# Two layers' expert entry: the last projection quarter in two pieces, and the picked rows formed in transposed order

## The chip, the cores and the metric

One Trainium2 chip, one of its cores. The metric is the device time of one launch in microseconds (us). The kernel before takes 2126.44 us (median of 3 runs, 2125.73 to 2127.97).

## The reference, cut to what matters

The program is two stacks of layers in one launch, all in fp32. The change touches only the second stack (256 latent tokens and 256 context tokens of width 1024, two layers), and in each of its layers only the passage from the mixer to the mixture of experts:

```python
# per layer: y_lat is the mixer's output (MLA in layer 0, short convolution in layer 1)
x = x + g1 * y_lat                                   # y_lat = heads @ w_o   (256 x 1024 @ 1024 x 1024)
f = rmsnorm(x) * g * (1 + sc2) + sh2
g_prob   = softmax(f @ w_group)                      # 4 groups
g_sel    = argmax(g_prob + b_group)
e_logits = (f @ w_expert)[g_sel]                     # 8 experts in the chosen group
e_prob   = softmax(e_logits); top-2 of e_prob + b_expert
# each token goes to 2 of 32 experts, whose weights are 3 x (1024 x 512) each:
y_e = (silu(f @ w_gate[e]) * (f @ w_up[e])) @ w_down[e]
x = x + g2 * sum over the two experts of weight * y_e
# after the second layer: rmsnorm(x) * final_g is the output (256 x 1024)
```

In both layers only the latent rows (256 tokens, so 512 assignments) go through the experts here, and all 32 experts' weights are read, 6 MB each.

## The kernel before, in words

**Entry** (`entry` in each engine's program, once per layer). The product with `w_o` is made in four quarters (token tile c of 128 rows, half h of 512 columns), each 8 matmuls deep, in order (0,0), (0,1), (1,0), (1,1), in banks 0 to 3. VectorE multiplies each quarter by the gate row and adds it to the residual (L2379, L2380). TensorE transposes the new rows of a quarter (`rows_T`, through `tr`, L870), ScalarE squares them for the norm (L1659) and copies the transposed rows to `hT` (L1836). The router's logits (`logits(c)`, 8 matmuls of 36 columns) need all of a tile's columns. In the last quarter (1,1) TensorE does, between its 4th and 5th k, the transpositions of (1,0) and the logits of tile 0 (`beside`). After the last quarter come its transpositions and the logits of tile 1. VectorE then has the two sums of squares added, the root, a diagonal `zdiag` for the normed rows of tile 1 (L2393), and from the logits (L2414, L2415) runs the routing, a chain of some 50 small instructions, up to the one-hot matrices of the first round (L2497, L2504).

**Experts** (`experts`). The 512 assignments are put in 48 blocks of 32 slots, each block of one expert; a round takes 3 blocks, so there are 16 rounds per layer. Turn b of TensorE is: gate product and up product (8 k each; of every k three matmuls of 32 stationary columns run side by side on the array, L1277 and L1279), forming of the next round's rows (`rows_of(b + 1)`, L1250: the one-hot matrix, 96 columns, is stationary and 512 columns of the normed tokens `fN` move; 2 halves x 2 token tiles, 4 matmuls, 8 records), transposition of the hidden rows (L1308), down product (4 k x 2 halves), and between its 2nd and 3rd k the transposition of the next round's rows (`rows_T(b + 1)`, L1261, 8 transpositions). The formed rows are copied from PSUM to `xe` in halves, one by ScalarE (L1791) and one by VectorE (L2492). The weights come straight from memory, where partition p holds rows 8p to 8p+7 of gate and up (4p to 4p+3 of down). So the stationary operand of chunk k has to hold the columns k, k+8, k+16, ... of the formed rows, and `rows_T` takes every eighth column of `xe` (`"t (p k) -> t k p"`) as the operand that is loaded: its words lie 32 bytes apart. The hidden rows (L1308) are read every fourth, 16 bytes apart. One product of the first stack also loads its weights with a stride: the compression takes `u[:, 0:31, j]`, words 64 bytes apart (the 128*31 loads of L856), while the 128*30 loads read `hid`, neighbouring words. No instruction of the kernel before moves an operand with a stride between its words.

**Weights of the experts.** Three experts lie in SBUF (`experts3`). SP issues 1 MB halves in a fixed order and waits before each for the quarter of the product that frees its place (`again`, L781). ScalarE and VectorE copy the weights of the second and third block of a round to a side buffer, a quarter at a time (L1780, L2538). The first round of a layer: rows formed, copied and transposed as a whole, then both copied to `xeT` (L1761), then the turn.

## Time and profile before

| | before |
|---|---|
| median of 3 runs | 2126.44 us |
| the profiled execution's own time | 2125.36 us |
| its span | 2123.5 us, 29332 instructions, mean granted clock 0.978 |
| PE busy | 1984.4 us (93%) |
| DVE busy | 992.9 us (47%) |
| ACT busy | 682.4 us (32%) |
| DMA moved | 619.89 MB, 292 GB/s on average |
| chain that ended last | PE 68%, DMA 24%, DVE 3%, ACT 2% |

Busy time is the union of an engine's instructions. The chain is followed back from the last instruction, at each step to what released it. The two layers of the second stack take the stretch from about 968 us to the end: entry and routing of layer 0 at 968 to 1002, its 16 rounds to 1478, the convolution and entry of layer 1 to 1632, its rounds to 2109.

### The profile page before, as it was taken

Reading aid. Unit: us, or ns where it says so; the run is one execution under the profiler, and the core shown is the slowest. Engines: PE = TensorE matmul, PEld = TensorE weight load, DVE = VectorE, ACT = ScalarE, POOL = GpSimd, SP = SyncE. Lnnn points to the kernel's source line nnn. Section 1 sums busy time; section 2 is a strip of 40 time slices with the busy share of each in tenths; the row PEclk is TensorE's granted clock in tenths of the full one; section 3 lists DMA queues with packets and bytes.
Section 4 is the critical chain, followed back from the end, with each engine's and each line's share of the span. In section 5 each row is a group of like instructions: output and inputs, shape, how many; then the busy total and the mean of one; then the engine's idle time right before and its main releaser. Section 6 shows DMA issues by size and latency. Waiting matters only on the chain.

```text
span 2123.5 us, 29332 instructions
## 1 busy us (share of the span) xinstructions
PE 1984.4 (93%) x9625; PEld 1080.3 (51%) x9626; DVE 992.9 (47%) x2203; ACT 682.4 (32%) x1092; POOL 45.0 (2%) x80
## 2 busy tenths in 40 slices
PE   8999999999999999999999888889998999888887
PEld 4536777646577775554433333334774333333333
DVE  2566886303398543444444333335224444333335
ACT  1451000103400003142555444444103554444444
POOL 2000000000000000000000000001000000000000
PEclk9999999998999999999999999999999999999999
DMA  9507995433289443305899999999555999999996
GB/s 306 210 7 290 362 346 220 159 119 140 106 343 366 149 165 136 122 37 201 351 414 422 419 416 422 423 423 367 218 198 210 400 419 423 422 423 422 422 422 256
DMA packets 78655, 619.89 MB, mean 292 GB/s; under 512 B 9664, under 2 KB 10000, under 8 KB 15712
## 3 DMA queue, kind: packets, MB, share of 16 engines
q1 hardware_dynamic: 67968, 540.51, 63.4%
q0 software_dynamic: 6944, 66.35, 8.2%
q10 hardware_dynamic: 3648, 11.89, 1.4%
q8 instruction: 44, 0.72, 0.1%
q14 instruction: 51, 0.42, 0.1%
HBM read 605.08 MB, written 13.63 MB: 291 GB/s over the span
## 4 chain that ended last, share of the span: by engine, by line
PE 68%; DMA 24%; DVE 3%; ACT 2%; issue 1%; DVEq 0%; SPq 0%; ACTq 0%; POOL 0%; POOLq 0%
PE ps L856 26%; DMA big<-in_w_up 21%; PE ps L1277 14%; PE ps L1103 14%; PE ps L1115 7%; PE ps L870 2%; PE ps L1250 2%; PE ps L1279 2%; DMA big<-in_w_gate 1%; DMA big<-in_w_down 1%; ACT big L1780 1%; PE ps L1261 1%; DMA big<-in_first_final_g 0%; DMA big<-in_dense 0%; PE ps L1125 0%
## 5 line engine op out<-in xcount | busy, mean ns | idle before, releaser
L1277 PE MATMUL ps<-big,hT 128*32 128x512 f32 x3072 | 698.2, 608 | 81.8 <-ACT big L1780 66.8
L1279 PE MATMUL ps<-big,hT 128*32 x1536 | 697.0, 608 | 0.0
L1780 ACT COPY big<-big 128x1024 f32 x384 | 395.6, 1046 | 494.2 <-PE ps L1279 269.6
L2538 DVE TENSOR_SCALAR big<-big 128x1024 f32 x384 | 262.1, 692 | 437.4 <-PE ps L1279 301.7
L1277 PEld LDWEIGHTS ps<-big,hT 128*32 128x32 f32 x3072 | 189.0, 111 | 459.9 <-issue 254.3
L1103 PE MATMUL ps<-hT,big 128*128 128x256 f32 x1408 | 311.2, 379 | 0.0
L856 PE MATMUL ps<-big,hT 128*128 128x512 f32 (+4 forms) x784 | 302.1, 537 | 3.4 <-ACT hT L1719 2.1
L1103 PEld LDWEIGHTS ps<-hT,big 128*128 128x128 f32 x1408 | 266.7, 190 | 49.4 <-issue 15.2
L856 PEld LDWEIGHTS ps<-big,hT 128*128 128x128 f32 x784 | 139.2, 192 | 131.7 <-issue 123.4
L1279 PEld LDWEIGHTS ps<-big,hT 128*32 128x32 f32 x1536 | 158.3, 111 | 3.7
L1115 PE MATMUL ps<-big 128*128 128x512 f32 x352 | 159.3, 595 | 0.7 <-DVE big L2302 0.7
L856 PE MATMUL ps<-big 128*128 128x512 f32 (+15 forms) x636 | 141.0, 451 | 13.8 <-issue 5.3
L2312 DVE SCALAR_TENSOR_TENSOR big<-big,s_ccol 128x512 f32<-128x512 f32 x196 | 147.4, 752 | 7.0
L1744 ACT ACTIVATE big<-big 128x256 f32<-128x256 f32 x44 | 18.3, 417 | 367.3 <-DVE big L2294 367.3
L1250 PE MATMUL ps<-big,hT 128*96 128x512 f32 x256 | 118.1, 604 | 1.2 <-DVE hT L2504 1.2
L856 PE MATMUL ps<-hT,big 128*128 128x256 f32 (+1 forms) x480 | 113.2, 397 | 1.9 <-ACT hT L2021 1.9
L856 PEld LDWEIGHTS ps<-big 128*128 128x128 f32 (+8 forms) x636 | 69.7, 176 | 79.8 <-issue 64.3
L856 PEld LDWEIGHTS ps<-hT,big 128*128 128x128 f32 x480 | 92.3, 193 | 23.7 <-issue 11.9
L1115 PEld LDWEIGHTS ps<-big 128*128 128x128 f32 x352 | 66.1, 190 | 73.5 <-issue 69.0
L2276 DVE TENSOR_TENSOR big<-ps,big 128x512 f32<-128x512 f32 x44 | 30.4, 690 | 115.4 <-PE ps L1103 114.6
L1250 PEld LDWEIGHTS ps<-big,hT 128*96 128x96 f32 x256 | 39.3, 163 | 78.0 <-issue 76.7
L2572 DVE TENSOR_TENSOR hT<-hT,ps 96x512 f32<-96x512 f32 x32 | 21.9, 683 | 88.6 <-PE ps L1279 88.6
(331 smaller groups left out, 1258.9 us busy)
## 6 DMA issues: line engine op xcount, KB each, us to landing
big<-in_w_gate SPq DMA_DIRECT2D x128, 1024.0 KB, 23.7
big<-in_w_up SPq DMA_DIRECT2D x128, 1024.0 KB, 23.2
big<-in_w_down SPq DMA_DIRECT2D x128, 1024.0 KB, 21.7
big<-in_dense SPq DMA_DIRECT2D x52, 1536.0 KB, 8.7
big<-in_dense POOLq DMA_DIRECT2D x28, 2048.0 KB, 9.9
big<-in_dense SPq DMA_DIRECT2D x20, 2048.0 KB, 7.9
y_rows<-c_res ACTq DMA_DIRECT2D x30, 384.0 KB, 7.0
big<-in_dense SPq DMA_DIRECT2D x7, 1024.0 KB, 31.7
```

What stands on the lines that cost most here:

```text
L856: ins = nc.tensor.matmul(out, lhsT, rhs, start=start, stop=stop)
L870: ins = nc.tensor.transpose(out, rows, const["ident"][0:k, 0:k])
L1103: ins = nc.tensor.matmul(ps[:, t % 2, f * S:(f + 1) * S], w[:, k, f * P:(f + 1) * P], hT[:, k, S:2 * S], start=k == 0, stop=k == KT - 1)
L1115: ins = nc.tensor.matmul(ps[:, 4 + 2 * c + h, :], gT[:, t % 2, c * P:(c + 1) * P], w[:, h * BW:(h + 1) * BW], start=t == 0, stop=t == FT - 1)
L1250: ins = nc.tensor.matmul(ps[0:ROWS, h, :], onehot[:, t, :], fN[:, t, h * BW:(h + 1) * BW], start=t == 0, stop=t == T - 1)
L1277: nc.tensor.matmul(ps[g * SLOTS:(g + 1) * SLOTS, bank, :], xT[:, k, g * SLOTS:(g + 1) * SLOTS], side[:, g - 1, quarter % 2, at:at + BW], s ...
L1279: return nc.tensor.matmul(ps[0:SLOTS, bank, :], xT[:, k, 0:SLOTS], experts3[:, bass.ds(here, 1), kind * CH + row:kind * CH + row + BW] .re ...
L1780: nc.scalar.copy(side[:, 1, quarter % 2, :], experts3[:, bass.ds(there, 1), lo:lo + QW] .rearrange("p a n -> p (a n)")).then_inc(s["side2_ ...
L2276: tt(U[:, par, :, 2:S + 2], ps[:, par, :].rearrange("p (a b) -> p a b", a=2), token_scale, mult)\
L2312: ins = stt(acc, mod_w[j % 2][:, k, :], ccols[:, k, col:col + 1], acc, mult, add)
L2538: ts(side[:, 0, quarter % 2, :], experts3[:, bass.ds(there, 1), lo:lo + QW].rearrange("p a n -> p (a n)"), 1.0, None, mult).then_inc(s["si ...
L2572: tt(hm[0:ROWS, :], sgm[0:ROWS, :], ps[0:ROWS, 3, :], mult).then_inc(s["hidden_done"].sem, 1)
```

## The change

The last quarter of the projection becomes two pieces of 256 columns, so that `PIECES` has five entries (tile, first column, width). TensorE makes piece 3, then the transpositions of piece 2 and the logits of tile 0 (both of its pieces), then piece 4 with the transpositions of piece 3 between its 6th and 7th k, then the logits of pieces 2 and 3, the transpositions of piece 4 and its logits. ScalarE squares and copies by pieces, VectorE adds the sums of squares of pieces 2 and 3 early and that of piece 4 in one instruction. `zdiag` moves behind the first two instructions of the routing.

In every round of the experts the rows are formed in transposed order: the 512 columns of `fN` that move are now four runs of 128 words, each run with a stride of 8 words (32 bytes), and `xe` is filled so that `rows_T` loads 128 neighbouring words for each transposition. `rows_T` waits for the two copied halves one after the other. In the first round of a layer ScalarE copies its half of the formed rows before its first copy of weights, VectorE its half after one copy of weights instead of two, and the turn begins when the first half of the transposed rows is there; the second half is awaited before k = 4.

```diff
...
 
+        PIECES = [(0, 0, BW), (0, BW, BW), (1, 0, BW), (1, BW, BW // 2), (1, BW + BW // 2, BW // 2)]
+        PIECE_BANKS = (0, 1, 2, 3, 2)
...
-                def product(c, h, between=None):
+                def product(i, between=None, at=4):
+                    c, lo, n = PIECES[i]
                     for k in range(KT):
-                        if between is not None and k == 4:
+                        if between is not None and k == at:
                             between()
-                        mm(ps[:, 2 * c + h, :], lhs(k, c), w[h][:, k, :], k == 0, k == KT - 1,
+                        mm(ps[:, PIECE_BANKS[i], 0:n], lhs(k, c), w[lo // BW][:, k, lo % BW:lo % BW + n], k == 0, k == KT - 1,
                            s["banks_ready"].sem if k == KT - 1 else None)
 
-                def rows_T(c, h):
-                    pe.wait_ge(s["dve_evac"].sem, s["dve_evac"].at(2 * c + h + 1))
-                    for k in range(4):
-                        tr(ps[:, 4 + 2 * c + h, k * P:(k + 1) * P], lat(c)[:, (4 * h + k) * P:(4 * h + k + 1) * P],
-                           e["turn_ready"].sem if k == 3 else None)
-
-                def logits(c):
-                    for k in range(KT):
-                        if k % 4 == 0:
-                            pe.wait_ge(e["turned_a"].sem, e["turned_a"].at(2 * c + k // 4 + 1))
+                def rows_T(i):
+                    c, lo, n = PIECES[i]
+                    pe.wait_ge(s["dve_evac"].sem, s["dve_evac"].at(i + 1))
+                    for k in range(n // P):
+                        tr(ps[:, PIECE_TURNS[i], k * P:(k + 1) * P], lat(c)[:, lo + k * P:lo + (k + 1) * P],
+                           e["turn_ready"].sem if k == n // P - 1 else None)
+
+                def logits(i):
+                    c, lo, n = PIECES[i]
+                    pe.wait_ge(e["turned_a"].sem, e["turned_a"].at(i + 1))
+                    for k in range(lo // P, (lo + n) // P):
                         mm(ps[:, c, 0:G + E], hT[:, k, S + c * P:S + (c + 1) * P], wrG[:, k, :], k == 0, k == KT - 1,
                            r["route_pe"].sem if k == KT - 1 else None)
 
                 def beside():
-                    rows_T(1, 0)
+                    rows_T(2)
                     logits(0)
-
-                product(0, 0)
+                    logits(1)
+
+                product(0)
                 pe.wait_ge(r["route_dve"].sem, r["route_dve"].at(1))
                 mm(ps[:, 3, 0:G + E], const["ones"][:], swS, True, True, r["route_pe"].sem)
-                product(0, 1)
-                rows_T(0, 0)
-                product(1, 0)
+                product(1)
+                rows_T(0)
+                product(2)
                 used()
-                rows_T(0, 1)
+                rows_T(1)
                 pe.wait_ge(r["route_dve"].sem, r["route_dve"].at(2))
-                product(1, 1, beside)
+                product(3)
+                beside()
+                product(4, lambda: rows_T(3), 6)
                 used()
-                rows_T(1, 1)
-                logits(1)
+                logits(2)
+                logits(3)
+                rows_T(4)
+                logits(4)
...
@@ -1247,17 +1260,17 @@
                         pe.wait_ge(s["xT_done"].sem, s["xT_done"].at(b * 2))
                     for h in range(2):
                         for t in range(T):
-                            ins = nc.tensor.matmul(ps[0:ROWS, h, :], onehot[:, t, :], fN[:, t, h * BW:(h + 1) * BW],
+                            ins = nc.tensor.matmul(ps[0:ROWS, h, :].rearrange("t (k p) -> t k p", k=4), onehot[:, t, :],
+                                                   fN[:, t, :].rearrange("t (p k) -> t k p", k=KT)[:, 4 * h:4 * h + 4, :],
                                                    start=t == 0, stop=t == T - 1)
                         ins.then_inc(s["rows_ready"].sem, 1)
 
                 def rows_T(b):
 
-                    pe.wait_ge(s["rows_copied_a"].sem, s["rows_copied_a"].at(b + 1))
-                    pe.wait_ge(s["rows_copied_v"].sem, s["rows_copied_v"].at(b + 1))
-                    for h in range(2):
+                    for h, copied in enumerate((s["rows_copied_a"], s["rows_copied_v"])):
+                        pe.wait_ge(copied.sem, copied.at(b + 1))
                         for k in range(4):
-                            rows = xe[0:ROWS, :].rearrange("t (p k) -> t k p", k=KT)[:, 4 * h + k, :]
+                            rows = xe[0:ROWS, (4 * h + k) * P:(4 * h + k + 1) * P]
                             ins = nc.tensor.transpose(ps[:, h, k * ROWS:(k + 1) * ROWS], rows,
                                                       const["ident"][0:ROWS, 0:ROWS])
                         ins.then_inc(s["xT_ready"].sem, 1)
@@ -1287,12 +1300,14 @@
                 def turn(b, first=False, more=True):
 
                     here = pe.value_load(tab_i[0:1, 0, bass.ds(b * WIDE, 1)], min_val=0, max_val=BPE - 1)
-                    pe.wait_ge(s["xT_done"].sem, s["xT_done"].at(b * 2 + 2))
+                    pe.wait_ge(s["xT_done"].sem, s["xT_done"].at(b * 2 + (1 if first else 2)))
                     if not first:
                         pe.wait_ge(s["hidden_done"].sem, s["hidden_done"].at(b))
                     for kind in range(2):
                         for quarter in range(4):
                             both_copied(b, 4 * kind + quarter)
+                            if first and kind == 0 and quarter == 2:
+                                pe.wait_ge(s["xT_done"].sem, s["xT_done"].at(2))
                             for k in range(2 * quarter, 2 * quarter + 2):
...
@@ -1755,8 +1770,8 @@
                 s = st[name]
                 done = s["quarter_done"]
 
-                def rows_T(b):
-                    for h in range(2):
+                def rows_T(b, halves=range(2)):
+                    for h in halves:
                         act.wait_ge(s["xT_ready"].sem, s["xT_ready"].at(b * 2 + (h + 1)))
                         nc.scalar.copy(xeT[:, 4 * h:4 * h + 4, :], ps[:, h, 0:4 * ROWS].rearrange("p (a b) -> p a b", a=4))\
...
                 there = third(0)
+                row_half(0)
                 copy(0, there, 0)
-                row_half(0)
+                rows_T(0, (0,))
                 copy(0, there, 1)
-                rows_T(0)
+                rows_T(0, (1,))
                 for b in range(ROUNDS):
...
-                            .then_inc(e["turned_a"].sem, 1)
+                for i, (c, lo, n) in enumerate(PIECES):
+                    act.wait_ge(s["dve_evac"].sem, s["dve_evac"].at(i + 1))
+                    nc.scalar.activation(sq_rest[:, min(i, 3), lo % BW:lo % BW + n], lat(c)[:, lo:lo + n], ACT.Square,
+                                         accum_out=ssq_pieces[:, i:i + 1]).then_inc(e["squares_done"].sem, 1)
+                    if i == 1:
+                        root_of(0)
+                    act.wait_ge(e["turn_ready"].sem, e["turn_ready"].at(i + 1))
+                    nc.scalar.copy(hT[:, lo // P:(lo + n) // P, S + c * P:S + (c + 1) * P],
+                                   ps[:, PIECE_TURNS[i], 0:n].rearrange("p (a b) -> p a b", b=P))\
+                        .then_inc(e["turned_a"].sem, 1)
                 root_of(1)
...
-                for c in range(TC):
-                    for h in range(2):
-                        i = 2 * c + h
...
+                def sum_of(i):
+                    v.wait_ge(e["squares_done"].sem, e["squares_done"].at(i + 2))
+                    link(v, tt(sums[:, 0:1], ssq_pieces[:, i:i + 1], ssq_pieces[:, i + 1:i + 2], add))
+                    link(v, ts(var[:, 0:1], sums[:, 0:1], 1.0 / D, EPS, mult, add))
+
+                for i, (c, lo, n) in enumerate(PIECES):
...
+                    v.wait_ge(s["banks_ready"].sem, s["banks_ready"].at(i + 1))
+                    link(v, tt(prodO[:, i % 2, 0:n], ps[:, PIECE_BANKS[i], 0:n], gate_row[layer][:, cols], mult))
+                    tt(out, out, prodO[:, i % 2, 0:n], add).then_inc(s["dve_evac"].sem, 1)
+                    if i == 2:
+                        link(v, stt(fN[:, 0, :], lat(0), rstd_x[:, 0:1], rowG, mult, mult))
...
-                ts(zdiag, const["ident"][:], rstd_x[:, 1:2], None, mult).then_inc(e["zdiag_done"].sem, 1)
+                        v.wait_ge(s["dve_evac"].sem, s["dve_evac"].at(i + 1))
+                        link(v, tt(fN[:, 1, cols], out, rowG[:, cols], mult))
+                    if i == 1:
+                        sum_of(0)
+                        root_of(e, 0, rstd_x[:, 0:1])
+                    if i == 3:
+                        sum_of(2)
+                nc.vector.memset(lg[:, 0:TC, G:], NEG)
+                v.wait_ge(e["squares_done"].sem, e["squares_done"].end)
+                link(v, stt(var[:, 0:1], ssq_pieces[:, 4:5], 1.0 / D, var[:, 0:1], mult, add))
+                root_of(e, 1, rstd_x[:, 1:2])
...
                 L(red(top, lg, ALU.max))
                 tt(ae, lg, wide(top, EPG), sub).then_inc(step, 1)
+                e = st["ent" + tag]
+                ts(zdiag, const["ident"][:], rstd_x[:, 1:2], None, mult).then_inc(e["zdiag_done"].sem, 1)
                 v.wait_ge(s["route_act"].sem, s["route_act"].end)
...
                         copy(b, there, loads, j, first)
-                        if j == 1 and first:
+                        if j == 0 and first:
                             row_half(s, 0)
```

## Rows read from the trace of the kernel before

**Rows 1.** Chain of waits, its longest pieces: start us, us, what

```profile
...
1025.21 3.60 PE ps L1250 x8
...
1051.67 3.60 PE ps L1250 x8
...
1440.77 3.60 PE ps L1250 x8
...
1453.42 17.30 DMA big<-in_w_down
...
1654.02 3.60 PE ps L1250 x8
...
2071.46 3.60 PE ps L1250 x8
...
```

**Rows 2.** Windows of layer 0: us, busy of each engine, PE clock, DMA share, GB/s

```profile
core 0: us, PE busy (x) PEld busy (x) DVE busy (x) ACT busy (x) POOL busy (x), PEclk, DMA share, GB/s
1010.00:1013.00 3.00, 3.00 (x18) 1.74 (x15) 0.68 (x1) 0.65 (x1) 0.00 (x0) 0.66 0.00 0
1020.00:1130.00 110.00, 108.36 (x683) 41.69 (x680) 48.27 (x85) 59.02 (x67) 0.00 (x0) 1.00 1.01 413
1330.00:1440.00 110.00, 96.18 (x588) 42.01 (x588) 42.51 (x75) 49.84 (x56) 0.00 (x0) 0.97 1.01 423
```

**Rows 3.** Groups of all instructions by shape: busy us, mean ns of one, idle before

```profile
...
L1250 PE MATMUL ps<-big,hT 128*96 128x512 f32 x256 | 118.1, 604 | 1.2 <-DVE hT L2504 1.2
...
L2921 DVE TENSOR_TENSOR big<-big,ps 128x256 f32<-128x256 f32 x8 | 3.4, 422 | 69.1 <-PE ps L856 69.1
...
```

**Rows 4.** Groups of weight loads by shape

```profile
...
L1261 PEld LDWEIGHTS ps<-c_ident,c_res 96*128 96x128 f32 x256 | 31.0, 204 | 28.7 <-issue 26.8 <-ACT c_res L1791 1.9
...
L870 PEld LDWEIGHTS ps<-c_ident,c_res 128*128 128x128 f32 x48 | 5.5, 140 | 2.1 <-issue 2.1
...
L856 PEld LDWEIGHTS ps<-big 128*31 128x31 f32 x64 | 2.4, 138 | 1.2 <-issue 0.4
...
L856 PEld LDWEIGHTS ps<-big 128*30 128x30 f32 x4 | 0.2, 107 | 0.8 <-issue 0.8
...
```

**Rows 5.** Timeline of a later round, the transpositions' weight loads

```profile
...
1033.22 0.97 PEld L1261 LDWEIGHTS ps<-c_ident,c_res 96*128 96x128 f32 x8 [0.84 <-issue]
...
```

**Rows 6.** Timeline of layer 1's entry: start us, us, instruction, idle before

```profile
...
1611.31 3.68 PE L856 MATMUL ps<-big 128*128 128x512 f32 x8
...
1615.10 0.69 DVE L2379 TENSOR_TENSOR big<-ps,big 128x512 f32<-128x512 f32 x1 [4.93 <-PE ps L856]
...
1616.55 0.63 ACT L1659 ACTIVATE big<-x_res 128x512 f32<-128x512 f32 x1 [6.16 <-DVE x_res L2380]
...
1617.06 1.92 PE L856 MATMUL ps<-big,hT 128*128 128x36 f32 x16
...
1618.70 0.29 DVE L2393 TENSOR_SCALAR big<-c_ident,rstd_x 128x128 f32<-128x128 f32 x1
...
1619.19 0.21 DVE L2414 SCALAR_TENSOR_TENSOR big<-ps,rstd_x,big 128x4 f32<-128x4 f32 x1
...
```

**Rows 7.** Timeline of layer 0's entry, the last logits

```profile
...
987.27 2.75 PE L856 MATMUL ps<-big,hT 128*128 128x36 f32 x16
...
990.06 0.22 DVE L2414 SCALAR_TENSOR_TENSOR big<-ps,rstd_x,big 128x4 f32<-128x4 f32 x1 [0.57 <-PE ps L856]
...
```

**Rows 8.** Timeline of layer 0's first round

```profile
...
1001.83 3.67 PE L1250 MATMUL ps<-big,hT 128*96 128x512 f32 x8 [1.16 <-DVE hT L2504]
...
1005.43 0.57 ACT L1791 COPY c_res<-ps 96x512 f32<-96x512 f32 x1
...
1005.74 0.68 DVE L2492 COPY c_res<-ps 96x512 f32<-96x512 f32 x1
...
1006.57 1.10 PE L1261 MATMUL ps<-c_ident,c_res 96*128 96x96 f32 x8 [1.07 <-DVE c_res L2492]
...
1008.46 0.94 PE L1277 MATMUL ps<-big,hT 128*32 128x512 f32 x2 [0.78 <-ACT hT L1761]
...
```

**Rows 9.** Timeline of layer 1's first round

```profile
...
1637.28 1.10 PE L1261 MATMUL ps<-c_ident,c_res 96*128 96x96 f32 x8 [0.87 <-DVE c_res L2492]
...
1638.96 0.62 PE L1277 MATMUL ps<-big,hT 128*32 128x512 f32 x2 [0.58 <-ACT hT L1761]
...
```

45 lines of the change are left out of this document (13 added, 32 removed).

## The prediction

> **What bounds the kernel now.** I read the chain of waits first. Through the experts of both layers it runs over TensorE's rounds at first and over the landing of weights later: rounds begin every 26.46 us at the start (1025.21 to 1051.67), while over 14 rounds the mean is (1440.77 - 1025.21) / 14 = 29.68 us in layer 0 and (2071.46 - 1654.02) / 14 = 29.82 us in layer 1 [rows 1]. The windows tell why. From 1020 to 1130 TensorE is busy 108.4 of 110 us, from 1330 to 1440 only 96.2 of 110, with the DMA engines fully busy at 423 GB/s [rows 2]. So transfers bound most rounds, and TensorE has 3.3 us to spare in a mean round and none in the first four or five. Two places are not covered by transfers. Between a layer's entry and its first round the DMA has nothing to do: 0 GB/s from 1010 to 1013, because the three places for experts are full until the first round frees one [rows 2]. What comes earlier there shifts the whole stream of transfers. The other is the last round: in layer 0 the chain still waits for w_down until 1453.42 + 17.30 = 1470.7, in layer 1 it is on TensorE from 2071.46 on [rows 1].
>
> The working is against the profiled execution, 2125.36 us (span 2123.5 and 1.9 around it), which stands 1.1 us under the median of 2126.44; differences carry over to the median unchanged.
>
> **Entry, both layers.** TensorE's order before the last piece is the same work: piece 3 and the first half of the old quarter both take 8 x 512 columns' time, since 16 records of 256 columns stand for 8 of 512, and the transpositions and 16 logit records between are the same. After the last product (ends 1611.31 + 3.68 = 1614.99) the old path is two VectorE instructions of 0.69 (1615.10 on), the squares (0.63, from 1616.55), the sums, the root, `zdiag` (0.29) and the logits' reading, of which the second tile's begins at 1619.19: 4.2 us [rows 6]. The new path: 256 columns take VectorE 0.42 instead of 0.69 [rows 3], twice, -0.54; the squares of 256 instead of 512 columns, -0.21 at the same proportion (an estimate); one small sum less, -0.19 (estimate, the spacing of such instructions); `zdiag` now runs where VectorE waits for ScalarE's exponential, about -0.2. Sum -1.1. The logits don't stand in the way: of the 16 records of 1617.06 (1.92 us) [rows 6] only the last 4 are left after the last copy, about 0.5 us, and they end near 1617.8, before the root. In layer 0 the old path also waited 0.57 for those logits, 2.75 us long at a lower clock [rows 7]; I take -1.5 there. Bounds: from 0 (the root alone sets the time and nothing shrinks) to -2.0. The second chunk of the projection's weights is also given back earlier, which only brings forward transfers whose data is not awaited.
>
> **First round, both layers.** Old, layer 0: rows formed 1001.83 to 1005.50, VectorE's copy to 1006.42, 8 transpositions from 1006.57, ScalarE's two copies, products from 1008.46 [rows 8]. New with rows formed at the old pace: VectorE's copy starts 0.1 earlier, at 1005.6, its transpositions run at 1006.4 to 1006.8 and TensorE goes straight on, since the first half is copied by then: products from 1006.9, -1.55. Layer 1: VectorE's copy already begins as the rows end; the transpositions of the second half end near 1637.7 and products start then instead of at 1638.96 [rows 9], -1.2. ScalarE's copy of weights moves behind its row copy by 0.57 [rows 8]; it is wanted at the first product, which leaves it 0.8 us. If that cover were gone it would cost at most those 0.57.
>
> **Rows formed by strided reading, 32 rounds.** Here the trace has no row of its own: no operand moves with a stride. The nearest rows are weight loads. A transposition's load of 128 neighbouring words takes 140 ns, of 128 words 32 bytes apart 204 [rows 4]: 0.50 ns more a word. For a product, which goes in fp32 at 2 cycles of the clock a word, 30 neighbouring words take 107 ns and 31 words 64 bytes apart 138 [rows 4]: about 0.97 ns more a word, twice the other. That is what a reader that fetches every word twice, and pays each time, would show. The moving side of the same product also takes 2 cycles a word: 8 records of 512 in 3.67 us [rows 3, 8], 0.43 us from one to the next. Paid twice a word it costs 512 x 0.97 = 0.50 us a record, 4.0 us for the 8 of a round. From throughput: 8 strided loads in 0.97 us, the last of them 0.20 long, are 0.110 us apart [rows 5], 0.86 ns a word; twice that is 0.88 us a record against 0.43, 3.6 us a round. Paid once, 0.25 a record, 2.0 a round. If the reader is fast enough for a word every two cycles, nothing. I take 3.5, near the product's own loads, and keep 0 and 4.0 for the range. The saving on the other side, 8 contiguous loads instead of strided ones, is at most 8 x 0.064 = 0.5 us a round and more likely 0.1, since the loads run beside the transpositions.
>
> The Trainium skill, "Advanced Engine Details and Errata", SBUF Cachelines, says that an access on another 16-byte line each time pays a penalty, and that two hits on a line are enough to absorb the latency. The rows on loads agree with the first half. By the second half, a record that fetches each word twice in a row would pay nothing; the 31-word load, if it fetches twice in a row, speaks against that. What it would make of the time is the first rival below.
>
> **What 3.5 us a round costs.** In the first round of each layer all of it is on the path. The start of the products then stands at -1.5 - 1.55 + 3.5 = +0.45 in layer 0 and -1.1 - 1.2 + 3.5 = +1.2 in layer 1. A TensorE-bound round becomes 26.3 + 3.5 - 0.1 = 29.7 to 29.9 us, against the means of 29.68 and 29.82: the slack of later rounds is gone, though little of the time is lost directly, 14 x 0.1 = 1.5 in layer 0, 0 in layer 1. With both at one pace each hiccup of either costs. In the TensorE-bound stretch transfers ran at 413 GB/s and not 423 [rows 2], 2.4% lost; if that held for some 340 us more of each layer, it were 8 us a layer. I take 2.5 a layer, 5 in all (bounds 0 and 16). In the last round the forming of round 15's rows at 2071.46 is on the path in layer 1: +3.5; in layer 0 it eats first what the wait for w_down leaves, +1.8 of 3.5. Sum: 0.45 + 1.2 + 1.5 + 5 + 1.8 + 3.5 = +13.5, so 2138.9 for the profiled execution and **2140** for the median. Its own range is 2130 (no coupling, and a price of 2.8) to 2153.
>
> **Rivals.**
> *The stride is free.* The words arrive in time for a 2-cycle pace. For it: three products run side by side on the array, so SBUF gives far more words than one stream asks; loads may have a shallower reader. Against it: the 31-word load. Then each layer's start shift is the whole effect, because the transfers follow it: -1.5 - 1.55 - 1.1 - 1.2 = -5.35, and the rounds' small saving is hidden under transfers: 2126.4 - 5.3 = 2121, range 2118 to 2123.5. This is the side of faster; it decides below a price of about 1 us a round.
> *Paid once a word.* 2.0 a round: first rounds -1.05 and -0.3; rounds of 28.2 stay under the transfers' 29.7; last rounds +2.0 and +0.5. Sum +1.2, 2127.5, range 2124 to 2130.
> *The halves don't do what they say.* If the second half's copy or ScalarE's later weight copy holds the first products, 1.0 us of each first round's gain is lost: +2 on any case; it changes no sign of the first and is in the ranges.
> *Coupling is hard.* With both servers at one pace and transfers issued strictly in order, 8 us a layer instead of 2.5: 2150, the top of the forecast's own range.
>
> **Chances.** The forecast (stride paid twice, with hard coupling in it) 0.56, free 0.31, once 0.13. What a measurement can tell from no change is 0.2%, 4.3 us: faster is under 2122.2, slower over 2130.7. The forecast is slower in 92 of 100 of its cases; free is faster in 87; once is mostly within. Slower 0.56 x 0.92 + 0.13 x 0.25 = 0.55, faster 0.31 x 0.87 + 0.02 = 0.29, same 0.16. For 8 in 10 the range takes in most of the free case: 2119 to 2151; the forecast's own is 2130 to 2153.
>
> **What would show it.** The records that form the rows: 0.43 us apart (free), 0.68 (once), 0.88 (twice), 8 of them 3.7, 5.5 or 7.2 us. The transpositions' loads at about 140 ns. The first products of a layer after its last rows record: 1.4 us instead of 3.0. From the end of the last product to the second tile's logits: 3.1 us instead of 4.2. TensorE-bound rounds of 29.8 instead of 26.4 and transfers over 1020 to 1130 below 413 GB/s. The prediction is wrong if the records keep their 592 ns, or if rounds lengthen and the layers' lengths don't: then transfers covered more than I count.

## The result, and the profile after

The changed kernel takes **2156.41 us** (median of 4 runs, 2151.95 to 2160.33) against 2126.96 for the kernel before, run beside it (2125.73 to 2127.97): slower by 29.5 us, a ratio of 1.0147 (95% interval 1.0125 to 1.0168). The forecast was slower, by 13.5 us, in a range from 2119 to 2151: the direction was right and the size was not. The profiled execution took 2160.33 us (span 2158.5), 4 us above its median.

First the price of the strided reading. These are the groups of all instructions by shape in the changed kernel (busy us, mean ns of one, idle before), which answer to [rows 3, 4]:

```profile
L1263 PE MATMUL ps<-big,hT 128*96 128x512 f32 x256 | 241.9, 1102 | 2.3 <-DVE hT L2527 2.3
...
L1274 PEld LDWEIGHTS ps<-c_ident,c_res 96*128 96x128 f32 x256 | 22.6, 141 | 29.4 <-issue 28.1 <-DVE c_res L2515 1.3
```

A record that forms rows takes 1102 ns instead of 604, and the loads of the transpositions 141 instead of 204. Then the chain of waits, the pieces that answer to [rows 1]:

```profile
1032.30 7.49 PE ps L1263 x8
...
1212.42 7.49 PE ps L1263 x8
1242.38 7.49 PE ps L1263 x8
...
1461.93 7.49 PE ps L1263 x8
...
1680.80 7.49 PE ps L1263 x8
...
2102.68 7.49 PE ps L1263 x8
```

The 8 records of a round take 7.49 us where they took 3.60, and a TensorE-bound round is 1242.38 - 1212.42 = 29.96 us long instead of 26.34. Fourteen rounds last 1461.93 - 1032.30 = 429.6 us in layer 0 (before 415.6) and 2102.68 - 1680.80 = 421.9 in layer 1 (before 417.4). Where in a layer the time goes is seen in windows cut where the rows of rounds 1, 8 and 15 are formed. The columns are the window's length, the busy time of each engine, PE's clock, the DMA share and GB/s. First the kernel before, the first two windows in layer 0, the last two in layer 1:

```profile
1025.10:1221.80 196.70, 186.32 (x1149) 73.18 (x1148) 83.30 (x147) 99.11 (x112) 0.00 (x0) 0.98 1.01 416
1221.80:1440.70 218.90, 192.62 (x1150) 84.07 (x1149) 83.38 (x147) 98.29 (x112) 0.00 (x0) 0.97 1.01 421
1654.00:1850.30 196.30, 186.05 (x1150) 74.95 (x1149) 83.18 (x147) 98.90 (x112) 0.00 (x0) 0.99 1.01 418
1850.30:2071.40 221.10, 192.73 (x1150) 84.47 (x1149) 83.29 (x147) 98.15 (x112) 0.00 (x0) 0.97 1.01 422
```

Then the same rounds of the changed kernel:

```profile
1032.20:1242.30 210.10, 208.54 (x1149) 70.06 (x1148) 83.28 (x147) 100.15 (x112) 0.00 (x0) 1.00 0.96 390
1242.30:1461.90 219.60, 211.96 (x1152) 74.92 (x1149) 83.56 (x147) 99.44 (x112) 0.00 (x0) 0.99 1.01 417
1680.70:1890.50 209.80, 208.23 (x1149) 68.14 (x1148) 83.28 (x147) 100.13 (x112) 0.00 (x0) 1.00 0.99 404
1890.50:2102.60 212.10, 209.06 (x1151) 70.26 (x1148) 83.35 (x147) 99.84 (x112) 0.00 (x0) 1.00 1.01 422
```

The loss stands in the first seven rounds of the stretch, 13.4 us in layer 0 and 13.5 in layer 1. There TensorE is now busy for 99% of the time, and the transfers drop from 416 to 390 GB/s and from 418 to 404. The work moved is the same in layer 0 (416 x 196.7 and 390 x 210.1 are both 82 MB). The later seven rounds take 0.7 us more in layer 0; in layer 1 they take 9.0 less, at 422 GB/s both times. There the transfers had run ahead: 404 x 209.8 is 84.8 MB against 418 x 196.3 = 82.1 before, and 2.7 MB are 6.4 us at 422 GB/s. Layer 1's chain of waits stays on TensorE up to 2040, so most of its later rounds are bound by TensorE too, at 29.96 us each. What sets the layers apart is mostly one round, layer 0's from 1212.4; this is it, and the same round of layer 1:

```profile
1212.40:1242.40 30.00, 29.79 (x167) 9.75 (x166) 11.90 (x21) 14.30 (x16) 0.00 (x0) 1.00 0.83 328
1860.70:1890.60 29.90, 29.69 (x165) 9.62 (x165) 11.89 (x21) 14.30 (x16) 0.00 (x0) 1.00 1.01 422
```

In layer 0's, the queue that issues the weights waits 18.7 us at one stretch for a place in SBUF that TensorE's products free; in layer 1's it is 8.9 us at most.

The rest of the profiled difference: 3.5 us lie ahead of layer 0's entry, where no instruction differs. I put them down to this execution: the traces of experiments 2, 3 and 4, with the same instructions up to there, stand 2.0 us later, 3.8 later and 0.6 earlier than the kernel before. From the first rows to the second rows of a layer it is +3.5 (26.85 against 23.31) and +5.0 (26.73 against 21.70); behind the last rows of layer 1 +3.8. The entry gained nothing in layer 0 and 1.7 us in layer 1. But the 1.7 us are not the shorter path of the pieces. Counted from the entry's first transposition, layer 1's products that count the experts' rows start at 26.83 us, before at 26.88; the gain lies behind them, 5.69 us to the first rows instead of 7.38, where the kernel before ran at half clock (1.2 of 2.4 GHz). First that stretch before, then in the changed kernel; the eighth number is the granted clock:

```profile
1626.80:1631.50 4.70, 4.68 (x8) 2.09 (x8) 3.32 (x20) 0.59 (x1) 0.00 (x0) 0.50 1.01 427
1649.90:1653.90 4.00, 2.94 (x16) 1.50 (x16) 3.40 (x20) 1.17 (x2) 0.00 (x0) 1.00 1.01 428
```

This stretch takes 6.4 to 7.4 us in layer 1 in the traces with the old entry (the kernel before and experiments 1, 5, 6, 7, 9 and 10) and 5.7 to 5.9 in those with the new one (the changed kernel and experiments 2, 3, 4 and 8). Why the clock differs there is open.

### The profile page after: what moved, and what is told of

Its sections match the earlier page's. It is cut to its first block, busy times and chain, and to the rows that moved or that the text cites. A ratio compares the mean times of both kernels' runs of the same rounds, so it can differ in the third digit from the quotient of the medians.

```text
span 2158.5 us, 29384 instructions
## 1 busy us (share of the span) xinstructions
PE 2083.4 (97%) x9657; PEld 1055.8 (49%) x9658; DVE 995.0 (46%) x2211; ACT 689.0 (32%) x1098; POOL 45.8 (2%) x80
## 4 chain that ended last, share of the span: by engine, by line
PE 86%; DMA 7%; DVE 3%; ACT 2%; issue 1%; SPq 0%; DVEq 0%; ACTq 0%; POOL 0%; POOLq 0%
PE ps L862 26%; PE ps L1290 25%; PE ps L1109 13%; PE ps L1263 9%; PE ps L1121 7%; DMA big<-in_w_up 6%; PE ps L876 2%; PE ps L1292 2%; PE ps L1274 1%; ACT big L1795 1%; DMA big<-in_first_final_g 0%; DVE hT L2602 0%; DMA big<-in_dense 0%; PE ps L1131 0%; PE ps L1323 0%
## 5 line engine op out<-in xcount | busy, mean ns | idle before, releaser
L1290 PE MATMUL ps<-big,hT 128*32 128x512 f32 x3072 | 680.7, 598 | 19.9 <-ACT big L1795 9.9
L1292 PE MATMUL ps<-big,hT 128*32 x1536 | 680.1, 598 | 0.0
L1290 PEld LDWEIGHTS ps<-big,hT 128*32 128x32 f32 x3072 | 184.3, 110 | 406.7 <-issue 253.6
L862 PE MATMUL ps<-big,hT 128*128 128x512 f32 (+5 forms) x800 | 302.5, 529 | 4.4 <-ACT hT L1734 2.1
L1263 PE MATMUL ps<-big,hT 128*96 128x512 f32 x256 | 241.9, 1102 | 2.3 <-DVE hT L2527 2.3
L862 PE MATMUL ps<-big 128*128 128x512 f32 (+14 forms) x652 | 145.0, 455 | 15.5 <-issue 4.9
L1292 PEld LDWEIGHTS ps<-big,hT 128*32 128x32 f32 x1536 | 155.9, 110 | 3.4 <-issue 0.7
L862 PEld LDWEIGHTS ps<-big 128*128 128x128 f32 (+7 forms) x652 | 75.3, 186 | 80.4 <-issue 62.3
L2602 DVE COPY hT<-ps 128x192 f32<-128x192 f32 x64 | 19.9, 352 | 157.0 <-PE ps L1323 157.0
## 6 DMA issues: line engine op xcount, KB each, us to landing
big<-in_w_gate SPq DMA_DIRECT2D x128, 1024.0 KB, 16.6
```

Of the source, the lines that this page charges most:

```text
L862: ins = nc.tensor.matmul(out, lhsT, rhs, start=start, stop=stop)
L1263: ins = nc.tensor.matmul(ps[0:ROWS, h, :].rearrange("t (k p) -> t k p", k=4), onehot[:, t, :], fN[:, t, :].rearrange("t (p k) -> t k p", k ...
L1290: nc.tensor.matmul(ps[g * SLOTS:(g + 1) * SLOTS, bank, :], xT[:, k, g * SLOTS:(g + 1) * SLOTS], side[:, g - 1, quarter % 2, at:at + BW], s ...
L1292: return nc.tensor.matmul(ps[0:SLOTS, bank, :], xT[:, k, 0:SLOTS], experts3[:, bass.ds(here, 1), kind * CH + row:kind * CH + row + BW] .re ...
```

## The experiments

All but the last two were timed against the kernel before on the same chip: its median was 2126.83 us beside experiments 1 to 4, 2126.42 beside 5 to 8 and 2125.37 beside 9 and 10.

### 1. The transposed order alone

The kernel before with this edit, and with the transpositions reading neighbouring words and waiting for the halves one after the other, as in the change; the entry and the first round's order stay as they were.

```diff
-ins = nc.tensor.matmul(ps[0:ROWS, h, :], onehot[:, t, :], fN[:, t, h * BW:(h + 1) * BW], ...
+ins = nc.tensor.matmul(ps[0:ROWS, h, :].rearrange("t (k p) -> t k p", k=4), onehot[:, t, :],
+                       fN[:, t, :].rearrange("t (p k) -> t k p", k=KT)[:, 4 * h:4 * h + 4, :], ...
```

> The kernel before with the transposed order alone: rows_of reads fN with stride 8 and the transpositions read xe contiguously; the entry and the first round as before. Theory A (the strided reading makes the loss): every round's rows records take 7.6 us instead of 3.7, TensorE-bound rounds last 30 us instead of 26.3, and the time is that of the changed kernel or a little more, since the small gains of the entry and the first round are missing: 2153 to 2160. Rival B (a third or more of the loss is from the entry's and the first round's new order, which moves the start of the weight transfers): 2137 to 2148.

Measured: 2156.47 us, ratio 1.014 (1.0124 to 1.0156). One of the change's three parts makes the whole loss. Rival B is out. The 14 rounds split as in the changed kernel: 429.7 us in layer 0 and 422.3 in layer 1.

### 2. The changed kernel without the transposed order

The edit of experiment 1 taken back in the changed kernel, its transpositions with it.

> The changed kernel with the contiguous rows and strided transpositions of before; pieces in the entry and the order of ScalarE and VectorE in the first round stay. Without the transposed order the first transpositions wait for both halves again. Theory A: the loss is gone, and what is left is the entry's gain on layer 1 (1.7 us) and little on layer 0: 2123 to 2128. Rival B: 2135 or more.

Measured: 2125.76 us, ratio 0.999 (0.9978 to 1.0002): no difference that can be told. In its trace the distance from the entry's first transposition to the first rows is 33.67 us in layer 0, before 33.63, and 32.52 in layer 1, before 34.25.

### 3. The same order, packed once a layer

`fN` is written in transposed order, so that the rounds read it contiguously.

```diff
+packed = lambda t: fN[:, t, :].rearrange("q (k p) -> q p k", k=KT)
+by_feature = lambda a: a.rearrange("q (p k) -> q p k", k=KT)
-link(v, stt(fN[:, 0, :], lat(0), rstd_x[:, 0:1], rowG, mult, mult))
+link(v, stt(packed(0), by_feature(lat(0)), rstd_x[:, 0:1], by_feature(rowG), mult, mult))
...
-link(v, tt(fN[:, 1, cols], out, rowG[:, cols], mult))
+link(v, tt(packed(1)[:, lo // KT:(lo + n) // KT, :], by_feature(out), by_feature(rowG[:, cols]), mult))
...
-mm(ps[:, 4 + h, :], const["ident"][:], rowS[:, cols], False, True, e["z_ready"].sem)
+mm(ps[:, 4 + h, :].rearrange("t (k p) -> t k p", k=4), const["ident"][:],
+   rowS.rearrange("t (p k) -> t k p", k=KT)[:, 4 * h:4 * h + 4, :], False, True, e["z_ready"].sem)
```

> The changed kernel, but fN is written once a layer in the transposed order (VectorE's operations of the entry write with stride, the z products read rowS with stride in two products), so that every round's rows products read contiguously; transpositions, pieces and halves as in the changed kernel. Theory A (the loss is the strided reading by TensorE, not the order itself): rows records 3.7 us again, rounds as before, first products of a layer about 1 us sooner: 2120 to 2127. Rival C (the strided access only moves: VectorE's 1024-wide operations take twice as long in the entry and the picks come later): 2128 to 2132. Rival B: 2137 or more.

Measured: 2126.38 us, ratio 0.9998 (0.9989 to 1.0007). The order costs nothing, the strided reading does: rows records are 3.67 us for 8 again, and TensorE-bound rounds 26.08 us, 0.26 shorter than before, because the transpositions' loads are contiguous (in a round that TensorE bounds, the passage around the 8 transpositions takes 1.33 us instead of 1.59, in experiment 2, with strided loads, 1.58). Rival C is true in small: VectorE's write into the packed rows, words 512 bytes apart, takes 1049 ns for 512 columns instead of 693, two z products read `rowS` with stride, and layer 0's first rows stand 35.06 us behind the entry's first transposition instead of 33.67 in experiment 2, layer 1's 33.82 instead of 32.52.

### 4. The register load ahead of the first transpositions

Experiment 3 showed why the halves gave so little in the first round. Its timeline in layer 0 (start us, us, instruction, idle before):

```profile
1011.52 0.55 PE L1274 MATMUL ps<-c_ident,c_res 96*128 96x96 f32 x4 [0.45 <-DVE c_res L2518]
1012.43 0.48 ACT L1776 COPY hT<-ps 128x384 f32<-128x384 f32 x1
1013.34 1.07 PE L1290 MATMUL ps<-big,hT 128*32 128x512 f32 x2 [1.27 <-ACT hT L1776]
```

The first half of the rows had been copied at 1011.59, and yet the products began 1.27 us after the last transposition. In this gap TensorE's queue holds the load of the expert's number, `here`, into a register, and the waits of `after` on semaphores of the entry and the routing.

```diff
+after(pe, "ent" + name[-1], "route" + name[-1], "g2_" + name[-1])
+here = expert_of(0)        # the value_load that stood at the head of turn(b)
 rows_T(0)
-after(pe, "ent" + name[-1], "route" + name[-1], "g2_" + name[-1])
-turn(0, first=True)
+turn(0, first=True, here=here)
```

> As the kernel with fN packed, and the first round's load of the expert's number into a TensorE register stands ahead of the first round's transpositions instead of behind them. Theory D (the halves gained nothing in the first round because this load then ended last, about 1.2 us behind the last transposition): first products 0.8 to 1.2 us after the last transposition sooner in each layer, time 0 to 2.4 us less than the packed kernel. Rival: ScalarE's second weight copy (1.05 us) ended last, and the products start no sooner.

Measured: 2123.62 us, ratio 0.9985 (0.9976 to 0.9995). The products start 4.93 us after the first rows instead of 6.28 and 6.17, in both layers: theory D, with 1.35 and 1.24 us a little more than its 0.8 to 1.2, and 2.8 us of time where it gave 2.4 at most. The edit moves the waits of `after` too, but they hold nothing: the first transpositions start 3.51 us after the first rows with and without them ahead. ScalarE's second weight copy still ends after that and holds nothing. The second rows of layer 0 follow the first by 19.84 us instead of 22.91, which is 3.1 us and not 1.3. The rest of it is the clock; layer 1, where experiment 3 already had the full clock, gains 1.3 (19.88 against 21.19). Windows of 6 us about the first products, in layers 0 and 1; the eighth number is the granted clock. Experiment 3:

```profile
1013.00:1019.00 6.00, 5.66 (x30) 2.76 (x33) 0.82 (x2) 1.20 (x2) 0.00 (x0) 0.72 0.01 3
1643.00:1649.00 6.00, 6.00 (x45) 3.28 (x42) 2.45 (x6) 2.77 (x3) 0.00 (x0) 1.00 0.25 61
```

The changed kernel:

```profile
1014.00:1020.00 6.00, 4.73 (x25) 2.50 (x26) 0.96 (x2) 2.03 (x3) 0.00 (x0) 0.72 0.01 3
1664.00:1670.00 6.00, 6.00 (x32) 3.26 (x35) 1.08 (x2) 1.45 (x2) 0.00 (x0) 0.72 0.00 0
```

Experiment 8, which has the same first round as this one:

```profile
1007.00:1013.00 6.00, 6.00 (x43) 1.97 (x45) 2.29 (x6) 3.46 (x5) 0.00 (x0) 1.00 0.54 176
1633.00:1639.00 6.00, 6.00 (x45) 1.94 (x48) 2.30 (x5) 3.45 (x5) 0.00 (x0) 1.00 0.51 178
```

Where the number is 0.72, TensorE works at half its clock (1.2 of 2.4 GHz) for part of the window. From first products to second rows it is then 16.6 to 16.8 us, and 14.9 to 15.1 at full clock: 16.7 in both layers of the changed kernel, 14.9 in both layers here, 16.7 and 15.0 in the kernel before. So layer 1 of the changed kernel lost 1.8 us in its trace. The gap alone does not decide it: experiment 3 has it in layer 1 at full clock (second line above), and so have layer 1 of experiment 1 and both layers of experiments 5 and 7, with products 3.2 to 3.5 us behind the start of the last rows record, where the changed kernel has 3.7 and 3.5. Of the 20 first rounds in the traces of the two kernels and of experiments 1, 2, 3, 5, 6, 7, 9 and 10, all with the gap, 10 are of the long kind; of the 4 without it, none. That the missing gap keeps the clock up is not shown by so few, and what decides stays open.

### 5 to 7. The same TensorE time without a stride, in three sizes

The kernel before, which forms some halves of the rows again over themselves. The edit for experiment 6; experiment 5 has `2 if h == 0 else 1` in place of 2, experiment 7 has `3 if h == 0 else 2`.

```diff
 for h in range(2):
-    for t in range(T):
+    for t in [t for _ in range(2) for t in range(T)]:
```

> The kernel before, where every round computes its first half of the rows twice (the second time over the first): 4 more contiguous records of 0.43 us, 1.72 us of TensorE a round, nothing strided and nothing else changed. Theory K (the two bounds alternate: a round lasts as long as the later of TensorE, 26.3 us plus what is added, and the transfers, 29.7 us on the mean): most of it lies beside transfers, 2128 to 2134. Theory L (each microsecond of TensorE costs the same share, 29.5 us for 30 rounds of 3.9 us, a quarter): 2127 + 0.25 x 30 x 1.72 = 2140.

> The kernel before with both halves of the rows computed twice: 3.44 us of TensorE a round in contiguous records. Theory A (what strided reading costs is only its TensorE time): close to the kernel with the transposed order alone (2156, which adds 3.9 us less 0.3 us), at most 0.2 us a round less: 2148 to 2156. Rival S (the strided reads also slow others, SBUF's port or the landing of transfers): 2140 or less, since these reads are contiguous. Theory L: 2153.

> The kernel before with the first half of the rows computed three times and the second twice: 5.16 us of TensorE a round. Theory K: TensorE bounds every round of 31.5 us, from here each further microsecond counts in full, 28 inner rounds of 31.5 against 29.75 and 2 to 6 us at the layers' ends: 2178 to 2186. Theory L: 2127 + 0.25 x 30 x 5.16 = 2166.

| TensorE a round, us | TensorE-bound round, us | time, us | against before, us | ratio (95%) |
|---|---|---|---|---|
| +1.72 | 28.05 | 2135.88 | +9.5 | 1.0046 (1.0031 to 1.0062) |
| +3.44 | 29.77 | 2152.60 | +26.2 | 1.0130 (1.0114 to 1.0145) |
| +3.62 (transposed order alone) | 29.96 | 2156.47 | +29.6 | 1.0140 (1.0124 to 1.0156) |
| +5.16 | 31.49 | 2198.19 | +71.8 | 1.0334 (1.0317 to 1.0350) |

Contiguous records of the same total cost as much as strided ones. Rival S is out: strided reading costs what its TensorE time costs, and no slowing of others is seen. The curve is no line: the first 1.72 us a round cost 9.5, the last 1.72 cost 45.6, which is 26.5 us for each microsecond, not far from the count of rounds, 32. For +1.72 theory K (2128 to 2134) was too low and theory L (2140) too high; for +5.16 both were too low. K has the kind of curve, and has it too flat.

### 8. The shift's products ahead of zdiag

Layer 0's entry in the changed kernel explains what became of its gain:

```profile
990.91 0.64 PE L862 MATMUL ps<-big,hT 128*128 128x36 f32 x4 [0.46 <-ACT hT L1851]
...
993.19 2.07 PE L862 MATMUL ps<-big 128*128 128x512 f32 x2 [1.64 <-DVE big L2443]
...
998.47 1.29 PE L862 MATMUL ps<-c_res,c_ident 128*128 128x512 f32 x2
999.69 0.62 PE L862 MATMUL ps<-c_ones,big 128*32 128x128 f32 x4
...
1000.42 0.28 DVE L2477 TENSOR_SCALAR big<-ps 32x128 int32<-32x128 f32 x1 [1.65 <-PE ps L862]
```

The logits are done at 991.5, `zdiag` comes at 993.1, four products of up to 2 us follow, and only behind them the counts (999.69), for which VectorE waits 1.65 us. The four products take 6.5 us because most of them run at half clock; in layer 1 of the kernel before they take 3.7 at full clock. On the packed kernel with the register load ahead:

```diff
-pe.wait_ge(e["zdiag_done"].sem, e["zdiag_done"].end)
 for h in range(2):
-    mm(ps[:, 4 + h, :], zdiag, fN[:, 1, cols], True, False)
-    mm(ps[:, 4 + h, :]..., const["ident"][:], rowS..., False, True, e["z_ready"].sem)
+    mm(ps[:, 4 + h, :]..., const["ident"][:], rowS..., True, False)
+pe.wait_ge(e["zdiag_done"].sem, e["zdiag_done"].end)
+for h in range(2):
+    mm(ps[:, 4 + h, :], zdiag, fN[:, 1, h * BW:(h + 1) * BW], False, True, e["z_ready"].sem)
```

> The packed kernel with the register load ahead, and the second tile's two products with rowS (identity by rowS) ahead of the wait for zdiag instead of behind it. Theory Z (the entry's gain in layer 0 was lost because the four z products, 6.4 us at half clock, start only when zdiag is there, and the products that count the experts' rows stand behind them on TensorE): counts 0.8 to 1.5 us sooner in layer 0, first rows 1 to 3 us sooner, 2120 to 2123. Rival: VectorE's chain of picks ends last there anyway; nothing gained, 2124.

Measured: **2118.04 us**, ratio 0.9965 (0.9952 to 0.9979), faster than both kernels. Its timeline in layer 0:

```profile
989.58 3.90 PE L862 MATMUL ps<-c_res,c_ident 128*128 128x512 f32 x4
...
993.30 1.90 PE L862 MATMUL ps<-big 128*128 128x512 f32 x4
...
995.99 0.62 PE L862 MATMUL ps<-c_ones,big 128*32 128x128 f32 x4 [0.79 <-DVE big L2473]
```

Now the counts wait for VectorE, no longer VectorE for the products. The time is below what theory Z gave it. From the entry's first transposition to the first rows it is 32.19 us in layer 0, against 33.63 before, and 32.18 in layer 1, against 34.25. That the -1.44 of layer 0 is so near the forecast's -1.5 is partly luck, for the clock differs as well. The stretch of the four products in the changed kernel, then here:

```profile
993.20:999.60 6.40, 6.40 (x8) 2.49 (x8) 4.88 (x24) 0.04 (x1) 0.00 (x0) 0.55 1.01 425
989.60:995.20 5.60, 5.60 (x10) 1.47 (x9) 4.84 (x25) 1.38 (x2) 0.00 (x0) 1.00 1.01 424
```

In layer 0 new order and full clock are not told apart. In layer 1 the order is seen by itself: the counts come 1.8 us sooner than in experiment 4 (26.27 against 28.11), at about the same clock over these products (0.74 and 0.75).

### 9 and 10. The added time in the early or in the late rounds alone

Experiment 6 again, with `times` at 2 in rounds 0 to 7 and 1 behind, and the other way round.

```diff
-    for t in range(T):
+    for t in [t for _ in range(times[0]) for t in range(T)]:
...
-with pe.Fori(1, ROUNDS - 1) as b:
+with pe.Fori(1, 7) as b:
+    turn(b)
+times[0] = 1
+with pe.Fori(7, ROUNDS - 1) as b:
     turn(b)
```

> The kernel before with both halves of the rows computed twice (3.44 us of contiguous records) in rounds 0 to 7 of each layer only. Theory T (the transfers bind the whole stretch; TensorE's added time is lost where it stops them, which is in the first rounds, where TensorE is the later one, and is absorbed where TensorE waits for them): most of the 26 us of the kernel with all rounds doubled: 2138 to 2150. Rival U (it costs the same wherever it stands): half of it, 2139.5 here and in the kernel with the late rounds alone, within 2 us of each other.

> The same in rounds 8 to 15 alone, where TensorE waits 2 to 6 us a round for transfers. Theory T: it lies in these waits, with 3.4 us for the last round of layer 1 at most: 2127 to 2134. Rival U: 2139.5.

Measured: early 2150.44 us, ratio 1.0112 (1.0088 to 1.0136), +25.1 us; late 2129.49, ratio 1.0016 (1.0005 to 1.0028), +4.1 us. Together they are 29.2 against the 26.2 of all rounds. Rival U (2139.5 for both) is out. Theory T holds for the late rounds; the early ones lie 0.4 us above its 2138 to 2150. What the split of the loop in two costs by itself was not measured; both have it. The windows between rounds 1, 8 and 15, with the early rounds lengthened, layer 0 and then layer 1:

```profile
1029.90:1238.40 208.50, 206.94 (x1206) 78.28 (x1205) 83.38 (x147) 99.95 (x112) 0.00 (x0) 1.00 0.96 393
1238.40:1455.20 216.80, 195.57 (x1151) 83.73 (x1148) 83.01 (x147) 98.40 (x112) 0.00 (x0) 0.95 1.01 421
1674.60:1883.50 208.90, 207.35 (x1206) 80.91 (x1205) 83.34 (x147) 99.99 (x112) 0.00 (x0) 1.00 0.99 405
1883.50:2098.10 214.60, 192.44 (x1149) 83.47 (x1149) 83.47 (x147) 98.41 (x112) 0.00 (x0) 0.97 1.01 422
```

The same with the late rounds lengthened:

```profile
1026.80:1223.60 196.80, 186.31 (x1150) 73.17 (x1149) 83.27 (x147) 99.13 (x112) 0.00 (x0) 0.98 1.01 416
1223.60:1443.10 219.50, 211.40 (x1205) 85.26 (x1204) 83.37 (x147) 99.10 (x112) 0.00 (x0) 0.98 1.01 416
1658.80:1857.60 198.80, 188.06 (x1150) 78.54 (x1149) 83.20 (x147) 98.89 (x112) 0.00 (x0) 0.98 1.01 417
1857.60:2074.70 217.10, 209.23 (x1205) 86.29 (x1204) 83.27 (x147) 98.83 (x112) 0.00 (x0) 1.00 1.01 422
```

Late, TensorE's busy time grows by 18.8 us in layer 0 (192.6 to 211.4) and the seven rounds by 0.6: it lies in waits for weights. (Layer 1's seven are even 4.0 shorter, behind early ones that are 2.5 longer though nothing in them was changed; whether that is the spread of single traces or the split of the loop is not known.) Early it grows by 20.6 (186.3 to 206.9), the rounds grow by 11.8, the transfers run at 393 GB/s, and the later rounds give back 2.1 of it in layer 0 and 6.5 in layer 1.

### 11 and 12. What a stride costs

The kernel before, whose four products read `fN` with four different strides; the rows formed are not those wanted, only the records' times are read. One run each, no comparison of the whole time.

```diff
+views = [words 8, 16, 32, 64 bytes apart]          # experiment 11
+views = [words 20, 24, 28 bytes apart, pairs of words every 32 bytes]   # experiment 12
+nc.tensor.matmul(out, onehot[:, t, :], views[2 * h + t], ...)
```

> The kernel before, whose four rows products read fN with four strides: words 8 bytes apart (first half, first tile), 16 (first half, second tile), 32 (second half, first tile) and 64 (second half, second tile); 512 words each, so the rows are not the reference's. Theory F (a record fetches pieces of 32 bytes and waits when each brings one word only): 0.43 us from record to record at 8 and 16 bytes, 0.92 at 32 and 64. Theory G (the price follows the bytes spanned): about 0.50, 0.64, 0.92, 1.5. Theory N (every reading that is not contiguous costs the same): 0.92 in all four.

> The same with words 20, 24 and 28 bytes apart (first half both tiles, second half first tile) and with pairs of neighbouring words every 32 bytes (second half, second tile); the rows are again not the reference's. Theory F: between 0.43 and 0.92, near 0.75 at 24 and 0.85 at 28 bytes, in proportion to the 32-byte pieces per word (5/8, 6/8, 7/8), and 0.46 for the pairs, which halve the pieces per word. Theory G: 0.71, 0.78, 0.85, and 0.92 for the pairs, which span the same bytes.

Each record's weights are loaded as the record before it starts, so the distance of two loads is the length of a record; two records make a product. Experiment 11, a round (start us, us, load, idle before):

```profile
1054.68 0.24 PEld L1256 LDWEIGHTS ps<-big,hT 128*96 128x96 f32 x2 [0.84 <-issue]
1055.21 0.16 PEld L1256 LDWEIGHTS ps<-big,hT 128*96 128x96 f32 x1 [0.29 <-issue]
1055.66 0.16 PEld L1256 LDWEIGHTS ps<-big,hT 128*96 128x96 f32 x1 [0.29 <-issue]
1056.54 0.18 PEld L1256 LDWEIGHTS ps<-big,hT 128*96 128x96 f32 x1 [0.72 <-issue]
1057.44 0.18 PEld L1256 LDWEIGHTS ps<-big,hT 128*96 128x96 f32 x1 [0.72 <-issue]
1058.36 0.18 PEld L1256 LDWEIGHTS ps<-big,hT 128*96 128x96 f32 x1 [0.74 <-issue]
1059.28 0.18 PEld L1256 LDWEIGHTS ps<-big,hT 128*96 128x96 f32 x1 [0.73 <-issue]
1060.14 0.20 PEld L1313 LDWEIGHTS ps<-c_ident,hT 96*128 96x128 f32 x1 [0.68 <-issue]
```

From one to the next: 0.53 and 0.45 us at 8 bytes, 0.88 and 0.90 at 16, 0.92 and 0.92 at 32, 0.86 at 64. Experiment 12, its last records:

```profile
1062.52 0.18 PEld L1257 LDWEIGHTS ps<-big,hT 128*96 128x96 f32 x1 [0.71 <-issue]
1063.43 0.18 PEld L1257 LDWEIGHTS ps<-big,hT 128*96 128x96 f32 x1 [0.73 <-issue]
1064.35 0.18 PEld L1257 LDWEIGHTS ps<-big,hT 128*96 128x96 f32 x1 [0.73 <-issue]
1064.82 0.20 PEld L1314 LDWEIGHTS ps<-c_ident,hT 96*128 96x128 f32 x1 [0.30 <-issue]
```

0.91 and 0.92 us at 28 bytes, and 0.47 for pairs every 32 bytes (20 and 24 bytes: 0.89 to 0.95). The first record of a round is a little longer whatever it reads, 0.51 instead of 0.43 in the kernel before, so that 8 bytes cost 0.02 us. None of the theories F, G and N as written holds. Full price begins at 16 bytes, so it is not the bytes spanned and not 32-byte pieces; at 8 bytes it is nearly nothing, so it is not every stride. All these readings fit one rule: the price is paid unless two words that are read one after the other lie within the same 16 bytes. A distance of 12 bytes, and pairs that start on other places, were not run.

## Why the prediction was right in direction and wrong in size

- **Rows formed by strided reading.** Right in kind, at the top of its bounds: 0.92 us from record to record, 3.9 a round, where I took 3.5 and kept 4.0 as the bound. Both workings from the trace's weight loads had given more than 3.5: 4.0 from the product's own loads, 3.6 from the spacing of the transpositions'. The transpositions' contiguous loads gave 0.26 a round, where I had 0.1.
- **The rival that the stride is free.** I gave it 0.31, and the runs put it out: two different words within 16 bytes take 0.45 to 0.53 us a record, one word alone 0.86 to 0.95. I had read the Trainium skill, "Advanced Engine Details and Errata", SBUF Cachelines, as if one word fetched twice counted as two hits. The runs agree with the page's 16-byte line if its two hits are two different words; that a penalty is paid then follows from it, while its size is not on the page and comes from the runs.
- **What 3.5 us a round costs: the step that failed.** I compared means: a round of 29.7 to 29.9 against means of 29.68 and 29.82, 1.5 us lost directly and 2.5 a layer for coupling, 4.0 and 2.5 in all. Measured +14.1 and +4.5. The mean hides two stretches. In the first seven rounds TensorE was already the later one in five of layer 0 and in four of layer 1, at 26.3 to 26.5 us a round, although the DMA engines were fully busy, and each further microsecond of it counts there; only in the later seven has it slack in every round (28.4 to 34.3 us). The runs with early and late rounds alone show it: 25.1 and 4.1 us. The rows for this stood in my own text: TensorE busy 108.4 of 110 us in the early window and 96.2 in the later one [rows 2], and even the words that it has nothing to spare in the first four or five rounds. A lengthened early round also holds up transfers, and what they lose in layer 0 (416 to 390 GB/s) its later rounds, mostly bound by transfers, don't make up. Layer 1 came out near the forecast (+4.5 against +2.5): 10.1 of the 12.1 us that the rounds lack are layer 0's. I had this as the rival of hard coupling, 8 us a layer, and put its price in the range's top and not in the sum.
- **Products of the first round.** I had -1.55 + 3.5 = +1.95 from first rows to first products in layer 0, and -1.2 + 3.5 = +2.3 in layer 1; measured +3.53 (10.16 against 6.63) and +3.25 (9.97 against 6.72). Of the 1.55 and 1.2 us that the halves should give, 0.4 and 0.6 came (3.9 less 3.53 and 3.25). I named a second copy or ScalarE's weight copy as what could hold them. It was a third thing: the register load, hidden before behind ScalarE's copies, stood bare. With it moved ahead the first products come 1.85 us after the start of the last rows record, where the kernel before has 3.55 and 3.14.
- **A term that was missing.** A granted clock at half through part of layer 1's first round: 1.8 us in the changed kernel's trace. Its cause stays open: experiment 1 has its products 3.51 us behind the start of the last rows record there, as late as the changed kernel's 3.50, and the full clock (15.0 us).
- **Entry.** Layer 1 -1.7 against -1.1, inside its bounds, but for another reason, so by luck: the path to the second tile's logits got 0.9 us shorter, the counts behind the z products came no sooner, and the 1.7 us are a stretch behind them that the kernel before ran at half clock. Layer 0 0.0 against -1.5: the path to the second tile's logits did get 1.5 us shorter, but the z products, whose `zdiag` the change moved behind the reading of those logits, set the end; `zdiag` itself comes 0.45 us later, 21.17 us after the first transposition against 20.72, and they take 6.5 us, mostly at half clock. I had counted that move as a gain and did not name what is queued behind its wait.
- **Last rounds.** +3.8 in layer 1 against +3.5; in layer 0 about +2.3 against +1.8.
- **The sum.** The profiled difference without the 3.5 us ahead of the entry is 31.5, 18.0 above the forecast (the medians differ by 29.5, 16.0 above it). The rounds, +18.6 against +6.5, are 12.1 of it, the halves and the stride's size 2.5, the clock 1.8, the entries 0.9, the last rounds 0.8.

Open stays why layer 0's round from 1212.4 waits so long for a place and layer 1's does not, so that layer 1 keeps 404 GB/s in its first rounds and gets 9.0 us back later while layer 0 gets none.

## What to carry to other kernels

Where two resources bound a loop in turn, price an added microsecond by stretch and not against the mean: here 3.44 us of TensorE a round cost 25 us in the first eight rounds of each layer and 4 in the last eight. A layout that a loop reads many times is best written once in the order in which it is read: packed, the same transposed order cost nothing (2126.4), read with stride 29.5 us. Before a wait is moved or shortened, list what stands behind it in that engine's queue, register loads too: on top of the packed order, two small moves of that kind made the fastest kernel of this case, 2118.0 (2126.4, then 2123.6, then 2118.0).

## What was not expected of the hardware

- A contiguous record of 512 fp32 words takes TensorE 0.43 us; words 8 bytes apart 0.45 to 0.53; at 16, 20, 24, 28, 32 and 64 bytes 0.86 to 0.95, without growing with the stride; pairs of neighbours every 32 bytes 0.47.
- A load into a TensorE register that stands bare ahead of products leaves about 1.3 us between them and the last transposition.
- VectorE writing 512 columns with words 512 bytes apart took 1049 ns against 693 contiguously: half as much again, where TensorE's reading doubles.
